# A table of expert gates built by accumulating scatters instead of one-hot matrix products, in a hybrid decoder step

## The reference

```python
qry = (h @ w_query).reshape(T, PEER_HEADS, 2, D_KEY_HALF)
sc = jnp.einsum('thpc,pnc->thpn', qry, sub_keys)
top_s, top_i = lax.top_k(sc, PEER_TOPK)
...                                  # the best 16 of 16 x 16 pairs, for each token and head
gate = jax.nn.softmax(best_s, axis=-1)
...
a = jnp.einsum('bd,bhkd->bhk', hb, u_tab[ib])
a = jax.nn.gelu(a, approximate=False) * gb
out = jnp.einsum('bhk,bhkd->bd', a, v_tab[ib])
```

## Time and profile before

| | us |
|---|---|
| median of 3 runs | 4578.69 (4576.86 to 4579.11) |
| span of the profiled execution | 4598.6 |
| PE busy, share of the span | 98% |
| DVE, ACT, POOL busy | 66%, 32%, 33% |
| stage of the one-hot products (chunks 20 to 55) | 1972 to 2414 |

### The profile page before, as it was taken

How to read it: one execution, slowest core, us unless ns; L and a number is a source line. 1 busy time by engine, 2 the same in 40 slices (tenths; PEclk the granted TensorE clock), 3 DMA queues, 4 the chain that set the end, 5 groups by cost and what they waited for, 6 DMA issues and landing times.

```text
span 4598.6 us, 79681 instructions
## 1 busy us (share of the span) xinstructions
PE 4519.9 (98%) x31465; PEld 4370.9 (95%) x31465; DVE 3019.9 (66%) x4190; ACT 1472.9 (32%) x2413; POOL 1495.7 (33%) x1076
## 2 busy tenths in 40 slices
PE   8999999999999999999999999999999999999998
PEld 8999999989999999988889999999999999999997
DVE  6643443334434779978883777664669989889843
ACT  4113332123323122267771121222233333332432
POOL 1000000010000004444443446243268777666311
PEclk9999999999999999999999999999999999999999
DMA  6555455455665545467777777776779899999522
GB/s 211 165 168 155 145 154 174 149 158 185 213 207 176 173 144 170 151 217 253 254 247 258 252 258 266 270 273 207 276 281 342 331 359 393 368 369 352 189 82 91
DMA packets 590447, 1044.65 MB, mean 227 GB/s; under 512 B 57633, under 2 KB 437809, under 8 KB 555441
## 3 DMA queue, kind: packets, MB, share of 16 engines
q1 hardware_dynamic: 230192, 510.99, 33.3%
q0 software_dynamic: 81808, 386.99, 22.5%
q10 hardware_dynamic: 278256, 144.08, 11.0%
HBM read 994.67 MB, written 274.86 MB: 276 GB/s over the span
## 4 chain that ended last, share of the span: by engine, by line
PE 87%; DVE 4%; DMA 3%; issue 2%; POOL 1%; ACT 1%; ACTq 0%; DVEq 0%; POOLq 0%; SPq 0%
PE PS L2326 55%; PE PS L2847 18%; PE PS L2350 10%; PE PS L2782 1%; DMA v_raw<-in_w 1%; DMA rows_y<-u_rows,sub_k 1%; DMA w_raw<-in_w 1%; DVE PS L2104 0%; POOL a_y L780 0%; DVE w_lo L1367 0%; PE PS L2726 0%; POOL a_el L830 0%; DMA rows_y<-v_rows,row_iy 0%; PE PS L2442 0%; ACT w_hi L896 0%
## 5 line engine op out<-in xcount | busy, mean ns | idle before, releaser
L2326 PE MATMUL PS<-h_hi,w_hi 128*128 128x288 f32 x6528 | 1955.3, 300 | 40.2 <-DVE w_lo L1367 25.0
L2326 PE MATMUL PS<-h_hi,w_lo 128*128 128x288 f32 x6528 | 1933.9, 296 | 0.0
L2326 PE MATMUL PS<-h_lo,w_hi 128*128 128x288 f32 x6528 | 1933.1, 296 | 0.0
L2326 PEld LDWEIGHTS PS<-h_hi,w_hi 128*128 128x128 f32 x6528 | 1235.1, 189 | 71.9 <-issue 36.1
L2326 PEld LDWEIGHTS PS<-h_lo,w_hi 128*128 128x128 f32 x6528 | 1235.8, 189 | 0.7
L2326 PEld LDWEIGHTS PS<-h_hi,w_lo 128*128 128x128 f32 x6528 | 1235.0, 189 | 0.0
L896 ACT ACTIVATE w_hi<-w_raw 128x1024 fp32r<-128x1024 f32 x444 | 470.6, 1060 | 1988.1 <-PE PS L2326 1904.8
L1367 DVE TENSOR_TENSOR w_lo<-w_raw,w_hi 128x1024 fp32r<-128x1024 f32 x404 | 499.0, 1235 | 722.9 <-ACT w_hi L896 718.8
L830 POOL DMA_INDIRECT a_el<-act_scr,act_i x192 | 336.4, 1752 | 59.1 <-issue 58.2
L2160 DVE SCALAR_TENSOR_TENSOR acc<-rows,a_sel,acc 128x2048 f32<-128x2048 f32 x128 | 301.3, 2354 | 7.4 <-DMA rows<-v_rows,row_i 4.6
L843 POOL DMA_INDIRECT rows<-v_rows,row_i x148 | 242.7, 1640 | 175.1 <-DVE acc L2160 101.1
(11 more groups left out here) (400 smaller groups left out, 7320.2 us busy)
## 6 DMA issues: line engine op xcount, KB each, us to landing
w_raw<-in_w SPq DMA_DIRECT2D x612, 512.0 KB, 4.7
v_rows<-in_w ACTq DMA_DIRECT2D x512, 256.0 KB, 3.9
v_raw<-in_w SPq DMA_DIRECT2D x128, 512.0 KB, 7.8
u_rows<-u_t SPq DMA_DIRECT2D x320, 128.0 KB, 3.6
act_scr<-gsp POOLq DMA_DIRECT2D x128, 288.0 KB, 4.2
gate_scr<-g_st POOLq DMA_DIRECT2D x12, 2048.0 KB, 8.4
k_raw<-in_w SPq DMA_DIRECT2D x40, 512.0 KB, 4.7
gates<-gate_scr SPq DMA_DIRECT2D x17, 768.0 KB, 7.3
```

Source lines behind the costliest of these rows:

```text
L2326: ins = mm(dst[:, a], w[:, m, at + n], xx[:, k, a * TH:(a + 1) * TH], start=first and n == 0 and r == 0, stop=last and n == len(ks) - 1 an ...
```

## The change

The one-hot products go, with the transposes of `gij`, the comparisons and evacuations on VectorE and the scalings on ACT. In their place:

- The table lies in DRAM as `g_rows`, one element for each expert chunk, key and token (`g_tok` is its view by chunk). In the output and query projections POOL clears it, 16 DMAs of 1536 KB from a tile of zeros, each let go by PE's progress.
- VectorE makes the element's place for each choice (`g_e`, `g_idx`, five small instructions in the index chain).
- POOL issues 384 indirect DMAs (`scatter`), each of 128 elements, one for each partition (token) of `gij`, which are added into `g_rows` in DRAM. They stand in chunks 21 to 59, 9 or 10 behind each `put`. A head's first scatter of a token tile waits for the landing of all scatters of the tile's heads before.
- The key blocks' low parts of the turned chunks from the fourth block on, and the first two blocks behind them, are made by VectorE (`key_low`), in turn with the transposes.
- T_PUT moves from 60 to 64 (a 16th fused group), the dots' gathers start at chunk 64 instead of 62, and the loads of `gates` and `fu_g` read 1536 or 1280 contiguous bytes a row.

```diff
-G_PUT = (UA + UG) // GRP + 1
+G_PUT = 16
-UR0, UR1 = UA, T_PUT
+UR0, UR1 = UA, 60
-S_AT = [62 + 23 * n // TS for n in range(TS)]
+S_AT = [64 + 21 * n // TS for n in range(TS)]
+ZC = 8
+TILES_G = TD // P
+N_SCAT = P * TILES_G
+SCAT_AT = [UA + 2 + 39 * n // N_SCAT for n in range(N_SCAT)]
...
                 if g == G_PUT:
-                    sp.wait_ge(S["g_ev"], 8 * ND + 2)
-                    for q in range(2):
-                        sp.wait_ge(S[f"gput{q}"], 16 * (ND // 2))
+                    for q in range(TILES_G):
+                        sp.wait_ge(S[f"scat{q}"], 16 * P)
                     sp.wait_ge(S["index"], 1)
...
-            pool.wait_ge(s_free_a, A_Q)
-            pool.dma_start(x_rows, x[:]).then_inc(S["x_again"], 16)
+            nc.gpsimd.memset(zeros[:], 0.0).then_inc(S["zero_set"], 1)
+            pool.wait_ge(S["zero_set"], 1)
+            for n in range(NK // ZC):
+                if n == NK // ZC // 2:
+                    pool.wait_ge(s_free_a, A_Q)
+                    pool.dma_start(x_rows, x[:]).then_inc(S["x_again"], 16)
+                pool.wait_ge(s_used, B_O + 2 + 4 * n - 4 * (n >= NK // ZC // 2))
+                pool.dma_start(g_tok[ZC * n:ZC * (n + 1)].rearrange("c p t -> p c t"),
+                               zeros[:].rearrange("p (c t) -> p c t", c=ZC)).then_inc(S["zeroed"], 16)
...
+            def scatter(n):
+
+                h, q, k = n // (TOPK * TILES_G), n // TOPK % TILES_G, n % TOPK
+                c = TOPK * h + k
+                if h and k == 0:
+                    pool.wait_ge(S[f"scat{q}"], 16 * TOPK * h)
+                pool.indirect_dma_start(g_rows, bass.IndirectOffsetOnAxis(ap=g_idx[:, q, c].unsqueeze(1), axis=0),
+                                        gij[:, q, 0, c:c + 1], None, compute_op=ALU.add
+                                        ).then_inc(S[f"scat{q}"], 16)
...
             puts(0, UA)
-            with pool.Fori(0, ND // 2) as i:
-                for u in range(2):
-                    for c in range(CG):
-                        put(UA + CG * u + c, [i], CG)
-                    pool.wait_ge(S["g_ev"], i * 16 + (8 * u + 10))
-                    pool.dma_start(d["g_scr"][i * 2 + u], g_st[:, u]).then_inc(S[f"gput{u}"], 16)
-            puts(UA + UG, T_PUT - UA - UG)
+            put(UA)
+            pool.wait_ge(S["zeroed"], 16 * (NK // ZC))
+            pool.wait_ge(S["index"], 1)
+            for u in range(3):
+                nc.gpsimd.memset(rows_y[:, u], 0.0).then_inc(S["axpy"], 1)
+            for t in range(UA + 1, T_PUT):
+                put(t, more=False)
+                for n in range(N_SCAT):
+                    if SCAT_AT[n] == t + 1:
+                        scatter(n)
...
+            dve.wait_ge(S["zeroed"], 16 * (NK // ZC))
...
+            def key_low(h, loops=()):
+
+                raw_b, hi_b, lo_b = k_slot(B_R0 + h)
+                dve.wait_ge(s_hi, at_step(B_R0 + h + 1, loops))
+                v.tensor_tensor(lo_b, raw_b, hi_b.bitcast(F32), ALU.subtract).then_inc(s_lo, 1)
...
+                for h in range(8, 12):
+                    key_low(h, [(i, 4)])
+                    u_turned(h, [(i, 4)])
...
-                        for q in range(4):
-                            ins = mm(PS[:, 2 * (n % 2) + q // 2, q % 2 * 256:q % 2 * 256 + 256], oh_j[:, n % 2, q],
-                                     oh_i[:, n % 2, q].rearrange("p r i -> p (r i)"), start=True, stop=True)
-                        ins.then_inc(S["g_mm"], 1)
```

More of the change, by code:

```diff
@@ L76 @@
 UA = 20
-CG = 3
-UG = CG * ND
 B_PG = B_U + 2 * NCHUNK
@@ L336, in build @@
         assert e <= rH
[L337 to L343, removed]
+        u_t3 = at("u_t3", [P, 4, 8, 32], F32, rZ + 5 * TB + 256)
+        assert rZ + 5 * TB + 256 + 4096 <= rZ + 7 * TB
         (raw3, whi3, wlo3, u_t0, u_t1, u_t2), e = run(
@@ L530, in _ @@
                     turned_out(B_R0 + u, [i])
-            for t in range(GATES_AT[0], NCHUNK - 1):
+            for t in range(UR1 - 1, NCHUNK - 1):
                 if t == UR1 - 1:
@@ L791, in row_y @@
                                         ).then_inc(S[f"row{m % 3}"], 16)
[L793 to L805, removed]
             for t in range(T_PUT, NCHUNK):
                 put_gated(t)
-                if t == UR1 + 2:
+                if t == T_PUT:
                     pool.wait_ge(s_used, B_R1)
@@ L1256, in value_high @@
                 nc.scalar.activation(v_slot(b)[1], v_slot(b)[0], ACT.Copy).then_inc(S["v_hi"], 1)
-            for t in range(UA + UG, NCHUNK - 1):
-                if t < UR1:
-                    for b in (B_U + 2 * t + 2, B_U + 2 * t + 3):
-                        (key_high if b < B_R1 else split)(b)
-                    gelu_prompt(t)
-                else:
-                    plain(t)
+            for t in range(UR1, NCHUNK - 1):
+                plain(t)
                 if t == S_DONE:
@@ L1920, in _ @@
             ch.did(v.tensor_reduce(part[:], f_one[:], AX.X, ALU.add))
+            ch.did(v.scalar_tensor_tensor(g_e[:], gij[:, 0:TILES_G, 1], float(NK), gij[:, 0:TILES_G, 2], ALU.mult, ALU.add))
             ch.wait()
+            ch.did(v.tensor_scalar(g_e[:], g_e[:], float(TD), part[:], ALU.mult, ALU.add))
+            ch.wait()
+            for q in range(TILES_G):
+                ch.did(v.tensor_scalar(g_idx[:, q], g_e[:, q], float(P * q), None, ALU.add))
             for r, tt, first in fix:
@@ L2052, in _ @@
+            for h in range(4):
+                u_turned(h)
+            dve.wait_ge(s_lo, B_R0 + 4)
+            for h in range(4, 8):
+                key_low(h)
+                u_turned(h)
+            with dve.Fori(0, (NU - 12) // 4) as i:
+                for h in range(8, 12):
+                    key_low(h, [(i, 4)])
+                    u_turned(h, [(i, 4)])
+            for h in range(NU - 4, NU):
+                key_low(h)
                 u_turned(h)
@@ L2058, in _ @@
                     ch.wait()
+            for b in (B_R1, B_R1 + 1):
+                split(b)
             def fused(g):
@@ L2202, in _ @@
                     fused(g)
-            dve.wait_ge(s_lo, B_U + 2 * T_PUT + 2)
-            for t in range(T_PUT, NCHUNK):
+            for t in range(UR1, NCHUNK):
                 turn = [("u", n) for n in range(TS) if S_AT[n] == t] + [("y", n) for n in range(NY) if Y_AT[n] == t]
@@ L2800, in plain_prompt @@
                     prompt_tile(t, range(8 * s, 8 * s + 8)).then_inc(s_used, 1)
-            plain_prompt(UA + UG)
-            pe.wait_ge(S["g_ev"], 8 * ND + 2)
+            with pe.Fori(0, (UR1 - 4 - UA) // 2) as i:
+                for u in range(2):
+                    plain_prompt(UA + u, [i])
+            plain_prompt(UR1 - 4)
+            pe.wait_ge(S["sc_f"], KD + 1)
             for k in range(KD):
@@ L2808, in _ @@
             ins.then_inc(S["hx"], 1)
-            for t in range(UA + UG + 1, UR1):
+            for t in range(UR1 - 3, UR1):
                 plain_prompt(t)
```

155 lines of the change are left out of this document (41 added, 114 removed).

## The result

The changed kernel takes 4848.8 us (median of 4 runs, 4845.1 to 4850.4), the kernel before beside it 4578.9: a ratio of 1.058, 95% interval 1.0565 to 1.0596. That is 270 us slower, where 44 were forecast; the direction was right, the size was not, and 4849 lies above the range.

The account below looks back on a forecast made before the run. PE was taken to bound the kernel before (87% of the chain), POOL's queue the changed stage: PE's gain of 50 us against POOL's path 94 us longer gives +44, so 4578.7 + 44 = 4623 us; range 4525 to 4740.

Parts of the forecast that it names:

- POOL's queue: POOL from the put of chunk 21 to that of chunk 60: scatters 499, puts 23, VectorE's low parts 37, together 559 us.
- 7.2: From the put of chunk 60 to PE's start of chunk 64, plus 0.6 for chunk 21's gelu ahead: 7.2 us.
- PE's 472: PE's time over chunks 22 to 63 if it waits for nothing: 472 us.
- What bounds the stage: Scatter stage: PE runs some three chunks ahead of POOL, then waits; POOL's path is 94 us longer.
- PE's 50 us: Prompt chunks 20 to 59: PE gains 50 us, 48 from the one-hot products and 2.4 from transposes of `gij`.
- The price of a scatter: Each of POOL's 384 scatters takes 1.30 us from start to start, 499 us in all.
- The rival of two reads: An accumulating scatter also reads the old value: 1.43 us each, 4673 us; chance 0.25 for this and somewhat more, to 4740.
- The dear rival: Scatters cost 2.05 us each, like the value stage's gathers: +295, 4874 us; chance 0.13.
- VectorE's low parts: 78 low parts moved to VectorE in 39 chunks hold up POOL's scatters 0.475 us each: 37 us, between 0 and 85.
- What costs nothing: Zeroing, added index instructions, SP's wait, VectorE's new work, the later first fused group and dots add nothing.
- Hidden after all: POOL's path hides behind PE, which keeps its 50 us: below 1.06 us a scatter, 4529 fully hidden; hidden or nearly, chance 0.17.
- the tie: The terms nearly cancel by chance: below 1.18 us a scatter, low parts at 37, the sum turns negative; chance 0.03.

Follow-up runs that it names:

- half the partitions: The changed kernel with each adding scatter taking 64 partitions in place of 128: 4811.8 us.
- not adding: The changed kernel with its 384 scatters writing their gate instead of adding it: 4650.0 us.
- gathers: The changed kernel with each scatter replaced by a gather with the same indices at the same place, into an unused buffer: 4634.6 us.
- not adding, half the partitions: The changed kernel with scatters that write and do not add, over 64 partitions in place of 128: 4589.5 us.
- low parts on POOL: The changed kernel with its adding scatters kept and the low parts of the turned key blocks made by GpSimd again: 5002.3 us.
- half the scatters: The changed kernel with 192 scatters in place of 384, spread over the same 39 chunks: 4541.6 us.

## Why the prediction was wrong in size

The sum of the prediction was: minus 50 for PE, plus POOL's queue from the `put` of chunk 21 to that of chunk 60, plus 7.2, minus PE's 472. With each run's own busy time and issue of the scatters in the queue, and 39 puts x 0.58 = 23, it can be worked out again for every run, and set beside the measured difference to the kernel before:

| kernel | scatters: busy + issue | POOL's queue | sum | measured |
|---|---|---|---|---|
| the change | 631.6 + 116.9 | 771.5 | +257 | +270 |
| half the partitions | 592.0 + 116.8 | 731.8 | +217 | +229 |
| not adding | 429.1 + 117.0 | 569.1 | +54 | +67 |
| gathers | 420.0 + 117.0 | 560.0 | +45 | +52 |
| not adding, half the partitions | 369.4 + 117.0 | 509.4 | -5 | +8 |
| low parts on POOL | 599.6 + 116.9 | 870.1, then 64.5 of PE | +413 | +421 |
| half the scatters | hidden behind PE | - | -50 | -41 |

In the row of the low parts on POOL the queue ends with the low part that PE waits for (2863.1 - 1993.0 = 870.1), PE's 64.5 us behind it stand in place of the tail, and of the 7.2 only the 0.6 at its start is left. The measured difference lies 7 to 14 us above the sum in every row, over a span of 460. So the structure held, point by point:

- **What bounds the stage.** POOL's queue, strictly in order, with PE some chunks ahead and then waiting for the low part: right, by the waits above and by the table.
- **PE's 50 us.** Half the scatters show 41, and the 10.88 us a chunk are there to the hundredth. The gelus of chunk 18 and chunk 80 tell where the rest is: before they start at 1957.95 and 2742.43, with half the scatters at 1953.75 and 2691.50. That is 47 us less, and in the other rows of the table, in their order, 263, 221, 57, 48 more, 4 less and 415 more: within 7 us of the sums. The other 4 to 12 us lie outside this stretch. The sums took PE's pace from an execution of the kernel before that is 20 us longer than its median; no trace here shows where a shorter one saves them. The gelu of chunk 80 before, then those of chunks 18 and 80 with half the scatters:

```profile
2742.43 0.63 ACT L1154 ACTIVATE gsp<-PS 128x576 f32<-128x576 f32 x1
```

```profile
1953.75 0.63 ACT L1171 ACTIVATE gsp<-PS 128x576 f32<-128x576 f32 x1
...
2691.50 0.63 ACT L1171 ACTIVATE gsp<-PS 128x576 f32<-128x576 f32 x1
```

- **The price of a scatter: the step that failed.** The prediction took 1.30 from start to start from the row gathers, on the ground that "an accumulating scatter also does one thing more per index" as a bounds check does. Undisturbed it is 1.552 + 0.304 = 1.86. The missing 0.56 x 384 = 213 us are the miss: +44 + 213 = +257. What was wrong in it is the unit. I looked for what the adding does to each index and scaled from a row with one more thing per index; the adding's price hangs mostly on the instruction (0.46 of 0.58 us, if it is a line), of which no row of the kernel before could show anything. Why it does, no run shows. The row with the bounds check also gathers rows of 2048 elements where the other gathers single ones, so what it takes more could not be put to the check alone. For an unseen operation with the nearest rows so far apart (0.88 to 2.05) I stood too close to the cheap end, and cut the range off below the dear one.
- **The rival of two reads** (1.43 a scatter, 4673) had the right cause, the adding, and a third of its price. The Trainium skill (Collectives: The Full Stack, section "The bandwidth ceiling") has, for the adding step of a ReduceScatter, two read descriptors a chunk of data where a copy has one. Taken over to the pieces of a scatter, as the rival did, that is a price by the element. Here only some 0.13 of the 0.58 us go by the element; the measurement decides, and the larger part has another cause, which no run shows.
- **The dear rival** (2.05 a scatter, 4874) came nearest: the mean with its issue is 1.645 + 0.304 = 1.95. But its row, the gathers of the value stage, is dear for another reason than this scatter: of the 192 gathers there the 19 that start while VectorE is idle take 0.95, the 85 that start inside its products with the value rows (L2160) 1.28 more each, while the scatter takes 1.54 at the least.
- **VectorE's low parts**: 37 us forecast, about 34 found. The rule behind the 37, a delay of what is left of the low part less 0.14, held: in the changed kernel 74 scatters start inside a low part and lose 34.2 us, where the rule gives 34.1; without the adding 81 do and lose 56.4, where it gives 56.2. Only the even spread was wrong, and that 37 is so close is luck. The first low part of a chunk shifts the scatters, and the second starts 2.30 us behind the first, so that it mostly falls at a fixed place of their turn: 0.66 us before the next scatter in the changed kernel (2216.04 and 2216.70 above), but 0.07 before it in the shorter turn without the adding, where it costs a scatter 0.99 us. The Trainium skill (SBUF — State Buffer, section "SBUF: two separate sides") lets the instruction that starts first hold the ports to its end; a VectorE instruction with two SBUF inputs does so only against one of GpSimd's that reads SBUF. For a low part that starts first the trace agrees, less the 0.14. The prediction's 1.23 us for each low part is not what that rule gives but its upper end, for one that starts right ahead of a scatter. The other way round the trace differs: a low part that starts inside a scatter is not held up (1.18 to 1.28 us, as elsewhere), and here the measurement decides. VectorE, then POOL, in the kernel without the adding:

```profile
2220.68 1.23 DVE L2005 TENSOR_TENSOR w_lo<-w_raw,w_hi 128x1024 fp32r<-128x1024 f32 x1 [10.42 <-ACT w_hi L1182]
...
2222.98 1.18 DVE L2005 TENSOR_TENSOR w_lo<-w_raw,w_hi 128x1024 fp32r<-128x1024 f32 x1
```

```profile
2221.05 1.70 POOL L765 DMA_INDIRECT g_rows<-gij,g_idx  x1 [0.31 <-issue]
2223.05 1.96 POOL L765 DMA_INDIRECT g_rows<-gij,g_idx  x1 [0.30 <-issue]
```

- **What costs nothing.** The zeroing, the five instructions more in the index chain, SP's wait and VectorE's longer work left no wait in the trace after that the sums lack; beside the zeroing, for one, the gelu of chunk 0 starts at 1726.6 us (before: 1728.9). The dots did cost something. PE's wait near the first fused group, put at nothing, is 15.6 us where it was 9.7 (gelus of chunks 65 and 66 after, 64 and 65 before, less 12.72), beside a dot that waits for its gathered key rows; in the other rows of the table it is 3 to 6 us longer than before. That is about what the sums lack between chunks 18 and 80 (2 to 6 us). The slower clock (0.85 in the stage) ate of PE's idle time, as foreseen: the `put`s keep their 20.2 us.
- **Hidden after all**: it takes 1.06 us a scatter or less by the prediction. At 0.892 + 0.305 = 1.20, and with the low parts 1.27 on average, the plain scatters of 64 partitions come out at +8 us, close to the tie that the prediction put at 1.18 and the low parts.

## What to carry to other kernels

Count the indirect DMAs that GpSimd must issue, before their elements: an indirect DMA of 4-byte elements took it 0.95 us and 0.30 of issue whatever its direction, an adding one 1.55 and 0.30, and 64 elements in place of 128 saved less than a tenth of that. Before moving work from a busy engine to an idle queue, divide the queue's spare time per step by that price (here five a chunk, and the change asked for ten). Where an operation that no row shows is the largest term of a sum, keep the dear row's end in the range.

## What the runs showed of the hardware that I had not expected

- The adding of an indirect DMA costs GpSimd 0.58 us over 128 partitions and 0.52 over 64, and in the records it lies behind the part that a plain scatter has too. The record of a `put` or a low part behind an adding scatter starts 0.96 to 0.99 us after the scatter's start, while the scatter's own still runs, and is longer by about the overlap. A `put` reads 1.19 to 1.21 us there instead of 0.59, and a low part on POOL, here in the timeline of the kernel with the low parts on POOL, 2.93 instead of 2.41. The queue pays nothing for it: the low part ends at 2227.19, and one of 2.41 behind the end of the scatter's record would end at 2227.23.

```profile
2223.27 1.55 POOL L765 DMA_INDIRECT g_rows<-gij,g_idx  x1 [0.30 <-issue]
2224.26 2.93 POOL L732 TENSOR_TENSOR w_lo<-w_raw,w_hi 128x1024 fp32r<-128x1024 f32 x1
```

- 384 scatters of 128 added elements, 49,152 in all, did not load the DMA engines: their share was 0.57 in the stage (0.76 before), and the puts behind them in the same queue landed in 3.0 us.
- VectorE's transposes, with one SBUF input, don't touch an indirect DMA: the 43 scatters that start inside one lose 0.15 us together. Its subtractions, with two, hold up a scatter that starts inside one until 0.14 us before their end.
